# Joining a residual stream from its rounded halves inside the expert loop and not behind it

## The reference

```python
u = rms_norm(h, norm_mix_g);  z = u @ w_in
ha = rg_lru(conv(z_a)) * gelu(z_y);  hb = multiscale_pool(z_b)
h = h + (gates_a * (ha @ w_up_a) + gates_b * (hb @ w_up_b)) @ w_out      # "h1" in the kernel
u = rms_norm(h, norm_ffn_g)
h = h + moe(u)            # 4 groups x 8 experts, top 1 group, top 2 experts, SwiGLU 1024 -> 512 -> 1024
u = rms_norm(h, norm_ple_g)                                             # h is "h2" here
h = h + sigmoid(u @ w_ple_gate) * (p @ w_ple)                           # "h3"
return rms_norm(h, final_norm_g)
```

## Time and profile before

| | |
|---|---|
| median of three executions | 893.72 us (893.7 to 894.01) |
| profiled execution | 892.15 us |
| span from first to last instruction | 890.4 us |
| mean granted clock of TensorE | 0.984 of full speed |
| TensorE busy | 838.7 us, 94% of the span |
| VectorE busy | 342.9 us, 39% |
| ScalarE busy | 272.0 us, 31% |
| scatters | 16, that is one round |

### The profile page before, as it was taken

How to read it: one execution, slowest core, us unless ns; L and a number is a source line. 1 busy time by engine, 2 the same in 40 slices (tenths; PEclk the granted TensorE clock), 3 DMA queues, 4 the chain that set the end, 5 groups by cost and what they waited for, 6 DMA issues and landing times.

```text
span 890.4 us, 10345 instructions
## 1 busy us (share of the span) xinstructions
PE 838.7 (94%) x4281; PEld 529.4 (59%) x4281; DVE 342.9 (39%) x478; ACT 272.0 (31%) x397; POOL 81.5 (9%) x61
## 2 busy tenths in 40 slices
PE   5999999999999999899999999899798897999996
PEld 4887888788888888435535354253352343533675
DVE  6899539962752616411020120101100101014954
ACT  7675336743332236202010100101001001013757
POOL 3427370000000000000000000000000000000000
PEclk9999999999999999999999999999999998999998
DMA  9222222211525763999999999999999999998802
GB/s 259 96 93 95 94 95 95 95 47 48 189 95 200 295 260 113 418 427 425 398 427 429 427 428 428 427 427 428 428 428 427 427 425 431 426 422 319 317 1 94
DMA packets 44758, 253.85 MB, mean 285 GB/s; under 512 B 8804, under 2 KB 9896, under 8 KB 31912
## 3 DMA queue, kind: packets, MB, share of 16 engines
q1 hardware_dynamic: 42120, 248.21, 68.6%
q0 software_dynamic: 2304, 4.20, 1.2%
q10 hardware_dynamic: 288, 0.79, 0.3%
HBM read 246.89 MB, written 10.49 MB: 289 GB/s over the span
## 4 chain that ended last, share of the span: by engine, by line
PE 70%; DMA 17%; DVE 6%; SPq 3%; ACT 2%; issue 2%; DVEq 0%; POOLq 0%; ACTq 0%
PE bank L1400 69%; DMA ring<-in_w_down_e_dram 11%; DMA ring<-in_w_up_e_dram 3%; DMA r<-in_w_ple_gate_dram 2%; DVE ring L1094 1%; PE bank L1610 1%; DVE ring L1074 1%; DMA ring<-in_w_in_dram 1%; SPq L514 1%; SPq L509 0%; SPq L607 0%; DVE r L1102 0%; ACT ring_rounded L397 0%; DVE ring L1100 0%; DMA expert_rows<-r,row_i 0%
## 5 line engine op out<-in xcount | busy, mean ns | idle before, releaser
L1400 PE MATMUL bank<-ring_rounded,ring_rounded 128*128 128x512 f32 (+1 forms) x696 | 245.6, 390 | 1.9 <-DVE r_rounded L1032 1.8
L1400 PE MATMUL bank<-r_rounded,ring_rounded 128*128 128x512 f32 (+1 forms) x744 | 234.5, 389 | 2.8 <-DVE ring_rounded L402 2.0
L1400 PEld LDWEIGHTS bank<-r_rounded,ring_rounded 128*128 128x128 f32 x744 | 138.8, 188 | 33.0 <-DVE ring_rounded L402 2.4
L1400 PEld LDWEIGHTS bank<-ring_rounded,ring_rounded 128*128 128x128 f32 x696 | 130.8, 188 | 29.8 <-DVE r_rounded L1032 2.5
L1400 PE MATMUL bank<-ring,gain 128*64 128x512 f32 x472 | 119.4, 610 | 10.7 <-issue 7.8
L1400 PE MATMUL bank<-ring,hT 128*64 128x512 f32 x400 | 110.6, 610 | 5.5 <-DMA ring<-in_w_down_e_dram 5.5
L1400 PE MATMUL bank<-ring,junk 128*64 128x512 f32 x472 | 115.4, 592 | 0.0
L1400 PEld LDWEIGHTS bank<-ring,gain 128*64 128x64 f32 x472 | 35.9, 140 | 79.0 <-issue 71.5
L1400 PEld LDWEIGHTS bank<-ring,junk 128*64 128x64 f32 x472 | 36.8, 137 | 72.3 <-issue 72.2
L1400 PEld LDWEIGHTS bank<-pick,r_rounded 128*128 128x128 f32 x576 | 71.1, 195 | 9.9 <-issue 8.5
L697 POOL DMA_INDIRECT expert_rows<-r,row_i x16 | 15.6, 977 | 670.0 <-DVE r L1294 670.0
(11 more groups left out here) (216 smaller groups left out, 766.0 us busy)
## 6 DMA issues: line engine op xcount, KB each, us to landing
ring<-in_w_up_e_dram SPq DMA_DIRECT2D x31, 2048.0 KB, 29.1
ring<-in_w_gate_e_dram SPq DMA_DIRECT2D x25, 2048.0 KB, 27.1
ring<-in_w_down_e_dram SPq DMA_DIRECT2D x22, 2048.0 KB, 31.8
ring<-in_w_in_dram SPq DMA_DIRECT2D x18, 1024.0 KB, 7.1
r<-in_w_down_e_dram SPq DMA_DIRECT2D x5, 2048.0 KB, 33.1
r<-in_w_gate_e_dram SPq DMA_DIRECT2D x5, 2048.0 KB, 27.8
ring<-in_w_down_e_dram SPq DMA_DIRECT2D x7, 1024.0 KB, 21.7
r<-in_x_dram SPq DMA_DIRECT2D x8, 512.0 KB, 8.1
```

The lines of the kernel that those rows point to most:

```text
L1400: return nc.tensor.matmul(*a, **k)
```

## The change

The stream is joined inside the expert loop. A new name, `h1_whole`, is ring slot 0 seen as four tiles. VectorE's `restore(n0, i)` waits until all gate and up products of the round are made, and writes tile `i` there as the sum of its halves. Three of these stand between `copy_hT` and `scale_y` of the last pair, and the fourth between `scale_y(14)` and `scale_y(15)`. The four restores behind the loop go. The first add of a tile reads `h1_whole` and writes `h1`; the second stays as it was. Since `gate_high(2)` writes into the same slot, ScalarE waits ahead of it until all four tiles have both adds. SyncE waits for the restores of a round before it loads the first matrix of another round into the slot, and ahead of the last gain for those of all rounds.

```diff
+        h1_whole = ring[:, 0, :].rearrange("p (i d) -> p i d", i=TT)
...
                         wait_expert_read(max(range(n, 3 * NE, LEAD)))
+                        if n == 0:
+                            sp.wait_ge(h1_restored, r * TT + TT)
                         load_expert(n)
...
             load_gate(3)
-            sp.wait_ge(h1_restored, TT)
+            sp.wait_ge(h1_restored, rounds * TT)
...
             norm_h2(0)
             norm_h2(1)
+
+            act.wait_ge(h2_ready, TT)
             gate_high(2)
             copy_h2T(2)
...
+            def restore(n0, i):
+                dve.wait_ge(gate_up_psum, n0 + PAIRS)
+                v.tensor_tensor(h1_whole[:, i, :].rearrange("p (q k) -> p k q", k=KD), rows_high(i), rows_low(i),
+                                ALU.add).then_inc(h1_restored, 1)
+
...
                         if m == PAIRS - 1:
                             copy_hT(n0, m)
+
+                            for i in range(TT - 1):
+                                restore(n0, i)
                         if m >= 1:
                             scale_y(n0, m - 1)
                         if m < PAIRS - 1:
                             copy_hT(n0, m)
+                restore(n0, TT - 1)
                 scale_y(n0, PAIRS - 1)
...
             dve.wait_ge(row_free, rounds * PAIRS + 1)
-            for i in reversed(range(TT)):
-                v.tensor_tensor(h1_by_k(i), rows_high(i), rows_low(i), ALU.add).then_inc(h1_restored, 1)
-                dve.wait_ge(h1_restored, TT - i)
+            dve.wait_ge(h1_restored, rounds * TT)
             def add_choice(i, k):
 
                 dve.wait_ge(y_in[k][i], 16)
-                ins = v.tensor_tensor(h1[:, i, :], h1[:, i, :], y_back(i, k), ALU.add)
+                ins = v.tensor_tensor(h1[:, i, :], (h1_whole, h1)[k][:, i, :], y_back(i, k), ALU.add)
```

## The result

The changed kernel takes 896.89 us (median of 9 executions, 894.83 to 898.78), the kernel before 893.2 us on the same chips (9 executions, 890.94 to 894.01). The ratio is 1.0048, 95% interval 1.0036 to 1.006: slower by some 4.3 us. (The ratio isn't the quotient of the two medians, which lie 3.7 us apart. The profiled execution took 895.31 us, span 893.6.

A forecast was written before the change was run, and what follows sets the result against it. The tail's chain from the last scatter through the gate-quarter transfer, ScalarE, VectorE and TensorE was taken as the bound. 0 (loop) + 1.0 (ScalarE's wait) - 0.2 (clock) = +0.8 us on 893.72: 894.5 us, range 892.3 to 896.5.

The forecast's parts named there:

- The restores are hidden in the loop: VectorE's four restores fit waits ahead of `scale_y(14)` and `scale_y(15)`, three using 6.15 of 6.34 us; costed at 0.
- The likeliest case: ScalarE waits for the last add ahead of `gate_high(2)`, third gate product 1.0 us later; +0.8 us, 894.5 us.
- Rival A: ScalarE's new wait doesn't bite, as adds are quicker or gate data later; 0.0, 893.7 us, chance 0.20.
- D: Rival: last scatter, freed of restores, lets tail transfers come up to 0.96 us earlier; 891.8 at best, chance 0.06.
- Rival B: TensorE's longer idle before the third gate product brings more low clock, up to 1.7 us; 896.4 us, chance 0.17.
- the term of the clock: TensorE behind the third gate product's wait: low stretch stays in place, less work falls into it; -0.2 us.
- that of the wait: ScalarE's `gate_high(2)` waits for the last add at 841.25, data there at 840.25; third gate product +1.0 us.
- The adds' end: VectorE's last add in the tail moves forward by about 1.2 us, from 842.43 to 841.25.
- A step costed at nothing: SyncE's added wait in the branch for a second round isn't executed, so it costs nothing.

The follow-up runs named there:

- e2: Changed kernel with ScalarE's wait for all four tiles moved from ahead of `gate_high(2)` to ahead of `gate_high(3)`; 893.02 us, ratio 1.0005.
- e3: Kernel before with only ScalarE's wait for the four tiles added ahead of `gate_high(2)`; 897.41 us, ratio 1.0071.
- e8: Kernel before, unaltered, run again for a second profile; 891.31 us.
- e11: Kernel before, unaltered, run again for a third profile; 892.1 us.
- e14: Kernel before with one more SyncE wait in the branch that isn't executed; 893.21 us, ratio 1.0009.
- e17: Kernel before, unaltered, run again for a fourth profile; 893.89 us.
- e12: Changed kernel with ScalarE waiting only for the four first adds ahead of `gate_high(2)`; 896.0 us, ratio 1.0037.
- e1: Changed kernel, unaltered, run again on another chip; 895.91 us, ratio 1.0046.
- e9: Changed kernel, unaltered, run again for another profile; 895.63 us.
- e10: Changed kernel, unaltered, run once more for another profile; 898.99 us.
- e13: Changed kernel with SyncE's extra instruction taken out: the wait for restores replaces the one for up products; 894.65 us, ratio 1.0036.
- e5: Changed kernel with 28 transposes of a constant tile filling TensorE's gap ahead of the third gate product; 893.6 us, ratio 1.0009.
- e4: Changed kernel with the wait ahead of `gate_high(3)`, `copy_h2T(2)` before `gate_high(2)` and `split_h2(2)` before `gate_low(2)`; 890.65 us, ratio 0.9984.
- e15: e4 with SyncE's extra instruction taken out as in e13; 890.28 us, ratio 0.9984.
- e18: Kernel before with only `copy_h2T(2)` ahead of `gate_high(2)` and `split_h2(2)` ahead of `gate_low(2)`; 889.76 us, ratio 0.9964.
- e19: e15 again, on one chip with e18; 890.94 us, ratio 0.9978.

## Why the prediction was wrong

**Right.** The restores are hidden in the loop, at 5.78 + 2.02 us with 0.64 and 4.18 us to spare. VectorE gains 8.2 us and spends them waiting for blocks. ScalarE's wait for the last add takes the place of the wait for the gate quarter and sets the tail; e2 takes that wait away and the loss with it, and e3 shows that it costs by itself. The likeliest case had the mechanism of the wait. Rival A fell (`gate_high(2)` starts at 26.5 to 28.6 us in all four profiles of the changed kernel, never on its data), and D fell: the last scatter doesn't get faster with the restores gone from beside it. From the last `scale_y` to the first load it is 4.3 to 5.2 us in the profiles with the restores in the loop and 4.4 to 5.2 us in those with them in the tail. Rival B gave 896.4 us, close to the measured 896.89, but that is luck: its second low stretch came in one profile of four, and its +1.0 us for the wait was as small as the forecast's.

The forecast was +0.8 us, and it was +4.3: 1.6 us of the difference lie in the term of the clock and 1.9 in that of the wait.

**The step that failed** is the one on the clock: "With the start 1.0 us later and the low stretch in the same place, up to 0.4 us less work falls into it; ... I take -0.2." It took the 1.7 us of the low stretch as paid by the kernel before in each execution. I had one profile, and it was the exception: one in four has the low stretch. At a gap of 1.3 us (e2, e8, e11, e14, e17) the clock fell in no profile; at 1.83 it did; at 2.76 us (e12) and 3.5 to 4.0 us (changed, e1, e3, e9, e10, e13) it fell in each. The term is +1.4 us and not -0.2, by the mean of four profiles each, and e5, which fills the gap and leaves the wait, brings the work behind it back to 41.94 us. The forecast and rival B both took a first low stretch as there already, so that only a second one would have a price; in fact the first one had it. (By the earlier trace rows that stretch lies from 847.5 to 850.9, and not from 847.3 to 850.8 as I read it; that changes nothing in the sum.) The Trainium skill ("TensorE: Matmul & The Clock Gate", Why this matters for your kernels) asks for no long idle gaps between bursts; the traces agree, with a fall behind each of seven gaps of 2.76 us or more, and here the rule should have had more weight than one row.

**A term mis-sized** is the wait itself, forecast +1.0 us up to the third gate product, measured +2.9 us. Two things are in it. The base: 31.74 us in the profile I had, 31.1 in the other three, because the gate quarter lands at 23.9 to 24.3 us there, so that VectorE's own adds (27.2 us) release `gate_low(2)`; that is 0.45 us on the mean. The adds' end: forecast at 26.13 us (841.25 less 815.12), measured at 26.4 to 28.5, mean 27.54: another 1.4 us. It comes from the second block, which I had landing at 9.9 us and which is added at 10.3 to 12.4.

**A step costed at nothing** stands behind part of that: "SyncE's for the second round isn't executed." It isn't, but it stands in SyncE's program, and the stall of the load issues moved by one issue (e13, e14). Its share of the time is 0.9 us by e1 and e13 (1.4 by the medians), 0.8 us by e14 and nothing by the ratios of e4 and e15. All of these are within the intervals, so it is not settled.

Open: why a 0.35 us later issue makes the landing 0.5 us later in some executions and 2.3 us in others; why e3 is 2.3 us (1.0 by the medians) above what its profile accounts for; and whether the restores' place costs the 1.2 us between e18 and e19.

## What to carry to other kernels

When a result is parked in a buffer to save one engine's time, look for who writes that buffer next, and let each writer wait for just the part that it overwrites: here the wait belonged one step later, and that made +0.48% into nothing that can be measured. Before a saving is counted, ask what the engine would wait for next; and before a cost is taken as already paid, look at more than one profile, above all where the clock is concerned: a gap behind which it rarely falls gets a second price when it grows. Here the real lever was the order of two operations on two engines that already stood ready, worth 0.26 and 0.36% in two measurements.

## What the hardware showed that I had not expected

A low stretch of TensorE's clock behind a gap costs 1.6 us (43.5 us of work behind the gap against 41.9), and once 2.4 us (44.36), where it lasted 6.8 us; with TensorE kept on constant transposes for 3.22 us it didn't come. The issue of a scatter on GpSimd that started 0.88 us behind a restore of VectorE took 1.85 us in place of 0.96, and one that started 0.16 us ahead of a restore took its 0.96. One instruction in a branch that is never taken moved a stall of 0.36 us in SyncE's load issues by one issue, in both kernels in which it was tried. The gate quarter's landing differed by 1.25 us between executions of one kernel (23.90 to 25.15 us behind the last `scale_y`).
